# Two MLP units interleaved at the start of the up projection, transpositions by pairs of token tiles, activation sums on VectorE

## The reference, cut to what matters

```python
mod = silu(c) @ w_mod + b_mod                   # shift2, scale2, gate2 are columns of it
x1 = x + gate1 * rms_norm(mixed @ w_out, g_post_mix)
h  = rms_norm(x1, g_pre_mlp) * (1 + scale2) + shift2
u  = relu(h @ w_mlp_up)                         # 2048 x 8192
y  = (u * u) @ w_mlp_down                       # 8192 x 2048
out = x1 + gate2 * rms_norm(y, g_post_mlp)
```

## Time and profile before

| | us |
|---|---|
| median of 3 runs | 2401.2 |
| lowest, highest | 2395.54, 2403.61 |
| profiled execution, its own time | 2401.67 |
| its span, first to last instruction | 2399.9 |
| TensorE busy (matmuls) | 2303.2 (96%) |
| VectorE busy | 1453.2 (61%) |
| ScalarE busy | 901.2 (38%) |
| GpSimd busy | 597.2 (25%) |
| mean granted TensorE clock | 0.979 |

### The profile page before, as it was taken

The page is one execution under the profiler, slowest core; times in us unless marked ns, Lnnn a source line. Parts: engine busy times, 40 slices in busy tenths (PEclk is TensorE's granted clock), DMA queues, the critical chain, the costliest instruction groups (busy, mean ns, idle before and its releaser), DMA issues.

```text
span 2399.9 us, 33914 instructions
## 1 busy us (share of the span) xinstructions
PE 2303.2 (96%) x13028; PEld 1940.1 (81%) x13028; DVE 1453.2 (61%) x1820; ACT 901.2 (38%) x1167; POOL 597.2 (25%) x348
## 2 busy tenths in 40 slices
PE   6989999999988999779999999999999999999998
PEld 1558787887767788679999999999888888888886
DVE  6649883992349564777777777776544333333335
ACT  4334424222336422644444444444322223222222
POOL 6544453444347000100000000001999300000000
PEclk8999999999999999899999999999999999999999
DMA  8977664333232475223333333334766545444433
GB/s 311 359 272 256 235 247 98 89 96 97 79 102 84 141 294 206 88 106 132 132 131 131 132 131 131 132 134 149 263 222 217 168 139 194 143 136 140 144 118 140
DMA packets 129760, 391.21 MB, mean 163 GB/s; under 512 B 18320, under 2 KB 19984, under 8 KB 117520
## 3 DMA queue, kind: packets, MB, share of 16 engines
q1 hardware_dynamic: 115408, 347.65, 41.9%
q10 hardware_dynamic: 9664, 25.70, 2.7%
q0 software_dynamic: 4608, 16.78, 2.4%
HBM read 356.25 MB, written 33.57 MB: 162 GB/s over the span
## 4 chain that ended last, share of the span: by engine, by line
PE 92%; DVE 5%; ACT 1%; issue 1%; DMA 1%; POOL 0%; DVEq 0%; ACTq 0%; SPq 0%; PEldq 0%; POOLq 0%
PE psum L852 29%; PE psum L854 29%; PE psum L853 29%; PE psum L932 1%; PE psum L917 1%; DVE steps L1775 1%; PE psum L894 0%; DVE pt_lo L2067 0%; DVE probs L2054 0%; ACT h_raw L1579 0%; DVE q_lo L2014 0%; DVE T_lo L2196 0%; PE psum L940 0%; DMA bias_s<-bias_out 0%; DMA pos_qi<-in_pos_columns 0%
## 5 line engine op out<-in xcount | busy, mean ns | idle before, releaser
L2139 DVE TENSOR_TENSOR w_lo<-raw,w_hi 128x1024 fp32r<-128x1024 f32 x128 | 175.7, 1372 | 425.1 <-ACT w_hi L1541 425.1
L854 PE MATMUL psum<-w_hi,uin_lo 128*128 128x512 f32 x1024 | 406.9, 397 | 0.0
L852 PE MATMUL psum<-w_hi,uin_hi 128*128 128x512 f32 x1024 | 406.1, 397 | 0.0
L853 PE MATMUL psum<-w_lo,uin_hi 128*128 128x512 f32 x1024 | 403.4, 394 | 0.0
L758 POOL TENSOR_TENSOR w_lo<-raw,w_hi 128x1024 fp32r<-128x1024 f32 (+1 forms) x96 | 260.6, 2719 | 338.3 <-ACT w_hi L1275 338.3
L1541 ACT ACTIVATE w_hi<-raw 128x1024 fp32r<-128x1024 f32 x128 | 135.6, 1060 | 491.4 <-PE psum L854 475.9
L852 PE MATMUL psum<-T_hi,w_hi 128*128 128x256 f32 x1024 | 290.1, 283 | 20.3 <-DVE T_lo L2196 20.3
L853 PE MATMUL psum<-T_lo,w_hi 128*128 128x256 f32 x1024 | 289.4, 283 | 0.0
L854 PE MATMUL psum<-T_hi,w_lo 128*128 128x256 f32 x1024 | 289.3, 283 | 0.0
L1275 ACT ACTIVATE w_hi<-raw 128x1024 fp32r<-128x1024 f32 (+1 forms) x128 | 129.2, 1013 | 348.4 <-PE psum L854 319.7
L852 PE MATMUL psum<-h_hi,w_hi 128*128 128x512 f32 (+1 forms) x592 | 238.7, 403 | 6.7 <-issue 4.0
(11 more groups left out here) (307 smaller groups left out, 4318.7 us busy)
## 6 DMA issues: line engine op xcount, KB each, us to landing
raw<-in_w_mlp_down SPq DMA_DIRECT2D x128, 512.0 KB, 3.9
raw<-in_w_in SPq DMA_DIRECT2D x88, 512.0 KB, 3.7
mod_ring<-in_w_mod_first SPq DMA_DIRECT2D x32, 1024.0 KB, 8.8
mod_slab<-in_w_mod SPq DMA_DIRECT2D x32, 1024.0 KB, 5.3
raw<-in_w_up_units SPq DMA_DIRECT2D x64, 512.0 KB, 5.1
unit_odd<-in_w_up_units SPq DMA_DIRECT2D x64, 512.0 KB, 4.8
uin<-u_s SPq DMA_DIRECT2D x128, 256.0 KB, 4.2
raw<-in_w_out SPq DMA_DIRECT2D x32, 512.0 KB, 5.8
```

The source lines that it names most:

```text
L852: nc.tensor.matmul(o, a_hi, b_hi, start=first, stop=False)
L853: nc.tensor.matmul(o, a_hi, b_lo, start=False, stop=False)
L854: return nc.tensor.matmul(o, a_lo, b_hi, start=False, stop=last)
L2139: V.tensor_tensor(w_lo[:, slot, :, :], raw[:, slot, :, :], w_hi[:, slot, :, :].bitcast(F32), ALU.subtract).then_inc(down_lo, 1)
```

## The change

- The tables of products have another order: A11 with B11, A12 with B21, then S1 with T1, S4 with B22, S3 with T3, S2 with T2, A22 with T4. (n, m) below counts in it.
- At the start, units 0 and 1 are taken together in the order `START`, 14 products over banks given by hand (`START_BANK`); unit 2 waits for the combinations that free them (`COMB_AFTER_START`).
- Each x1 tile has its own root and diagonal: one `rsqrt` for tiles 0 and 1, one for 2, one for 3 (`x1_scales`). The transpositions go in four groups of 16: group 0 and 1 are tiles 0 and 1 with lower and upper feature tiles (B11, B21), group 2 and 3 tiles 2 and 3 (B12, B22). ScalarE reads quadrants, 256 wide, 32 reads in place of 16.
- All T sums are VectorE's. GpSimd has no work here.
- Weight sums are in place: S3 over A21, S2 over A11, S4 over A12, S1 in one of two buffers. P1 has two buffers; the combinations write straight into `u_st`; five of the seven come together after product 5 (the sixth).
- SyncE loads unit 1 once the output projection has ended, unit 2 after the low part of operand (0, 6).
- The start of the down projection asks for its banks in the order of the new products.

```diff
-OP_A = ("A11", "S1", "S2", "A12", "S3", "S4", "A22")
-OP_B = ("B11", "T1", "T2", "B21", "T3", "B22", "T4")
+OP_A = ("A11", "A12", "S1", "S4", "S3", "S2", "A22")
+OP_B = ("B11", "B21", "T1", "B22", "T3", "T2", "T4")
+SUMS = ("S1", "S3", "S2", "S4")
+T_SUMS = ("T1", "T3", "T2", "T4")
+TURNED = ("B11", "B21", "B12", "B22")
+START = ((0, 0), (0, 1), (1, 0), (1, 1), (0, 2), (1, 2), (0, 3), (1, 3), (0, 4), (0, 5), (0, 6), (1, 4), (1, 5), (1, 6))
+START_BANK = {(0, 0): 4, (0, 1): 5, (1, 0): 6, (1, 1): 7, (0, 2): 4, (1, 2): 5, (0, 3): 6, (1, 3): 7, (0, 4): 0, (0, 5): 1,
+              (0, 6): 2, (1, 4): 3, (1, 5): 0, (1, 6): 1}
+START_COMB = ((1, 3, 4, 5, 6, 7, 8), (2, 9, 10, 11, 12, 13, 14))
 N_SUMS = 4
 N_COMBS = 7
-COMB_OF = (0, 5, 1, 3, 4, 6, 7)
+COMB_OF = (0, 1, 5, 6, 3, 2, 7)
+COMB_AFTER_START = (9, 14, 8, 10, 6, 12, 7)
...
-        diag = at(32, "diag", [P, TT, P], F32)
+        diag = at(0, "diag", [P, TT, P], F32)
...
+        def place(n, m, i):
+            return START.index((n, m)) if at_start(i) and n < 2 else OPS * n + m
+        def operand(p, i):
+            return START[p] if at_start(i) and p < 2 * OPS else divmod(p, OPS)
+        def comb_no(n, k, i):
+            if at_start(i) and n < 2:
+                return START_COMB[n][k - 1]
+            return i * (BLOCK * N_COMBS) + (N_COMBS * n + k)
+        def op_bank(n, m, i):
+            b = START_BANK[n, m] if at_start(i) and n < 2 else m
+            return psum[:, 4 * (1 - TURN_HALF) + b if b < 4 else 4 * TURN_HALF + b - 4, 0:TOK]
+        def turn_bank(group, b):
+            return psum[:, 4 * (TURN_HALF if group == 1 else 1 - TURN_HALF) + b, :]
...
-            for t in range(TT):
+            def store_x1(t):
                 sp.wait_ge(x1_ready, t + 1)
                 sp.dma_start(x1_s[:, t, :], y1[:, t, :]).then_inc(x1_stored, 16)
-            load_quad(1, Q11)
-            load_quad(1, Q21)
-            sp.wait_ge(t_pool, 4)
-            load_quad(1, Q22)
-            load_quad(1, Q12)
-            for n in range(2, BLOCK):
-                load_unit(n, 0)
+            store_x1(0)
+            store_x1(1)
+            sp.wait_ge(slab_used, MLP0)
+            for qd in (Q11, Q12, Q21, Q22):
+                load_quad(1, qd)
+            store_x1(2)
+            store_x1(3)
+            sp.wait_ge(op_lo, START.index((0, OPS - 1)) + 1)
+            for qd in (Q21, Q22, Q11, Q12):
+                load_quad(2, qd)
+            load_unit(3, 0)
...
-            for hf in range(2):
-                k = slice(HALF // 2 * hf, HALF // 2 * hf + HALF // 2)
-                pool.wait_ge(h_full_ready, KD)
-                pool.wait_ge(t_ready, 2)
-                nc.gpsimd.tensor_tensor(h2_quad["T3"][:, k, :], h2_quad["B22"][:, k, :], h2_quad["B12"][:, k, :],
-                                        ALU.subtract).then_inc(t_pool, 1)
...
+            def turn(group):
+                first, kt0 = 2 * (group // 2), HALF * (group % 2)
+                if group == 0:
+                    pe.wait_ge(dve_freed, freed("D", STAGE["mod4"] + 1))
+                if group == 1:
+                    pe.wait_ge(act_freed, a0)
+                    pe.wait_ge(dve_freed, d0)
+                for t in range(first, first + 2):
+                    pe.wait_ge(diag_ready, t + 1)
+                    for kk in range(HALF):
+                        kt, b = kt0 + kk, kk // 2
+                        if group >= 2 and t == first and kk % 2 == 0:
+                            pe.wait_ge(h_full_ready, 2 * HALF * (group - 2) + 2 * b + 2)
+                        c = TOK * (kk % 2) + P * (t - first)
+                        last = nc.tensor.matmul(turn_bank(group, b)[:, c:c + P], y1[:, t, P * kt:P * kt + P], diag[:, t, :],
+                                                start=True, stop=True)
+                        if t > first and kk % 2:
+                            last.then_inc(turned, 1)
+            def product(n, m, i):
+                p = place(n, m, i)
+                pe.wait_ge(op_lo, i * (BLOCK * OPS) + p + 1)
+                if at_start(i) and n < 2:
+                    if (n, m) == (0, 0):
+                        pe.wait_ge(h_full_ready, 2 * HALF)
+                    elif START_BANK[n, m] < 4 and m < 5:
+                        pe.wait_ge(h_full_ready, 4 * HALF)
+                    elif (n, m) in ((0, 2), (0, 3)):
+                        pe.wait_ge(p1_ready, m - 1)
+                    elif (n, m) in ((1, 2), (1, 3)):
+                        pe.wait_ge(comb_ready, comb_no(m - 2, 1, 0))
+                    elif (n, m) == (1, 5):
+                        pe.wait_ge(comb_ready, comb_no(0, 3, 0))
+                    elif (n, m) == (1, 6):
+                        pe.wait_ge(comb_ready, comb_no(0, 2, 0))
+                elif at_start(i) and n == 2:
+                    pe.wait_ge(comb_ready, COMB_AFTER_START[m])
+                elif m == 0:
+                    pe.wait_ge(p1_ready, i * BLOCK + n)
+                else:
+                    pe.wait_ge(comb_ready, comb_no(n - 1, COMB_OF[m], i))
+                o = op_bank(n, m, i)
+                    if at_start(i) and n == 0 and k % (HALF // 2) == 0:
+                last.then_inc(op_used, 1)
...
-            pe.wait_ge(diag_ready, TT)
-            for kt in range(HALF + HALF // 2):
-                turn_x1(kt)
-            def turn_beside(k):
-                if k < HALF // 2:
-                    turn_x1(HALF + HALF // 2 + k)
-            product(0, 0, 0, after=turn_beside)
-            for m in range(1, OPS):
-                product(0, m, 0)
-            for n in range(1, BLOCK):
+                last.then_inc(op_used, 1)
+            turn(0)
+            turn(1)
+            turn(2)
+            product(0, 0, 0)
+            product(0, 1, 0)
+            turn(3)
+            for n, m in START[2:]:
+                product(n, m, 0)
+            for n in range(2, BLOCK):
...
-                for t in ((2, 3, 0, 1), (0, 1, 2, 3))[TURN_HALF]:
+                for nth, t in enumerate(((2, 0, 3, 1), (0, 2, 1, 3))[TURN_HALF]):
                     if j == 0:
-                        pe.wait_ge(comb_ready, N_COMBS * UNITS - {2 * TURN_HALF: 1, 2 * TURN_HALF + 1: 0}.get(t, 2))
+                        pe.wait_ge(comb_ready, N_COMBS * UNITS - (6, 4, 1, 0)[nth])
...
+            for kk in range(HALF // 2):
+                h_full_of(0, kk)
+            x1_squares(TT - 1)
+            for kk in range(HALF // 2, HALF):
+                h_full_of(0, kk)
+            b_high(0, 0)
+            b_high(0, 1)
+            for p in range(2):
+                op_high(*START[p], 0)
+            for kk in range(HALF):
+                h_full_of(1, kk)
+            b_high(1, 0)
+            b_high(1, 1)
+            for p in range(2, RING):
+                op_high(*START[p], 0)
+            for kk in range(HALF):
+                h_full_of(2, kk)
             for hf in range(2):
-                for k in range(HALF // 2 * hf, HALF // 2 * hf + HALF // 2):
-                    h_full_of(k)
-                b_high(0, hf)
-            for k in range(HALF, HALF + HALF // 2):
-                h_full_of(k)
-            for hf in range(2):
-                b_high(1, hf)
-            for k in range(HALF + HALF // 2, KD):
-                h_full_of(k)
-            after_product(0, 0, 0)
-            for m in range(2, OPS):
-                for hf in range(2):
-                    b_high(m, hf)
-                after_product(0, m - 1, 0)
-            after_product(0, OPS - 1, 0)
-            for n in range(1, BLOCK):
+                b_high(2, hf)
+            for p, (n, m) in enumerate(START):
+                after_product(n, m, 0)
+                if p == 2:
+                    for kk in range(HALF):
+                        h_full_of(3, kk)
+                if 2 <= p <= 5:
+                    for hf in range(2):
+                        b_high(p + 1, hf)
+                if p == START.index((1, 4)):
+                    finish_unit(0, 0)
...
-                    out, a, b, op = s_tmp[0][:], a21, a22, ALU.add
+                    if not at_start(i) or n >= 2:
+                        dve.wait_ge(op_lo, ops + OPS * n - 8)
+                    V.tensor_tensor(s1, a21, a22, ALU.add).then_inc(s_ready, 1)
                 elif k == 1:
-                    out, a, b, op = s_tmp[1][:], s_tmp[0][:], a11, ALU.subtract
+                    V.tensor_tensor(a21, a11, a21, ALU.subtract).then_inc(s_ready, 1)
                 elif k == 2:
-                    out, a, b, op = a21, a11, a21, ALU.subtract
+                    dve.wait_ge(op_lo, ops + place(n, 0, i) + 1)
+                    V.tensor_tensor(a11, s1, a11, ALU.subtract).then_inc(s_ready, 1)
                 else:
-                    dve.wait_ge(op_lo, ops + 2)
-                    out, a, b, op = s_tmp[0][:], a12, s_tmp[1][:], ALU.subtract
-                if k:
-                    dve.wait_ge(s_ready, at_)
-                V.tensor_tensor(out, a, b, op).then_inc(s_ready, 1)
```

(63 more changed lines are left out.)

261 lines of the change are left out of this document (102 added, 159 removed).

## The result

| | before | changed |
|---|---|---|
| median (lowest to highest) of 8 runs each, us | 2399.45 (2393.93 to 2406.62) | 2379.46 (2373.99 to 2389.08) |
| ratio, 95% interval | | 0.9924 (0.9904 to 0.9944) |
| profiled execution: own time, span | 2401.67, 2399.9 | 2383.34, 2381.5 |
| mean granted clock | 0.979 | 0.985 |

A second comparison, of 6 runs with 11 of the kernel before, gave 2381.28 against 2395.91, ratio 0.9937 (0.9919 to 0.9954): 14.6 us.

The account below looks back on a forecast made before the run. TensorE, busy 96%, bounds, with time to win in start-up holes behind other engines. The 21st product moves from 1088.4 to 1077.2, 11.2 us, taken as 10: 2401.2 becomes 2391.0 us, range 2385 to 2398.5.

Parts of the forecast that it names:

- ScalarE term: ScalarE's queue before product (0,0): 16.4 us from 977.4, reads 0.48 each; start at 993.9, 4.6 us before the old one.
- term of unit 2's weights: At unit 2's start: A11 lands at 1047.9, A12 at 1049.2; (2,0) starts at 1055.8 instead of 1053.0.
- subtraction of 1.3: On the whole start: the old queues laid out alike end 1.3 us too early, so 11.2 us gain became 10.
- The other price that the prediction gave: ScalarE's 256-wide reads under the Read-Write Bubble: if each cost its whole duration, the sum would be 3.1 us longer.
- All sums on VectorE: VectorE bounds from B22 on; moved T3 and T4 sums cost some 4.6 us; 14th product ends at 1053.1.
- But that alone gives little: Diagonals per tile: the 9.85 us hole shrinks to 1.1, with little gain alone because ScalarE becomes the first bound.
- rival 3: TensorE in the new start: half clock stays, 16 us slower, 2417.5; 4 in 100, shared with a loop acquiring waits.
- rival 4: At the start: more than laid out, the holes go and half clock with them, gain over 15 us; 5 in 100.
- signs of being wrong: Loop over 19.94 us a unit, first product after 996, VectorE instructions over 1.25 us, clock at 0.5 beyond 1045.

Follow-up runs that it names:

- B22 read earlier: Changed kernel with ScalarE reading B22's transpositions two weight operands earlier; stretch 96.43 us against 98.65.
- late loads: Kernel taking units 0 and 1 one after the other, with two of unit 1's weight quarters issued only after T4's sums; stretch 104.21 us against 97.80.
- three reorderings: Changed kernel with B22 read earlier, unit 1's last three weight sums before B22's low part, unit 2's quarters each behind its operand; stretch 91.77 us, ratio 0.9925 to before.
- units one after the other: Changed kernel with unit 0's seven products, then unit 1's, in place of interleaved; stretch 97.80 us against 98.65.
- one weight copy early: Kernel with three reorderings, one weight high part before the last tile's squares, unit 0's first weight sum after the first tile's addition; stretch 92.07 us against 91.77.

## Why the prediction was wrong

The time lies 11.5 us below the forecast of 2391.0. The sum was 4.3 too small: the ScalarE term, the term of unit 2's weights and the subtraction of 1.3 are the steps that failed, each about 1 us. The starting level was 1.75 too high. The remaining 5.7 (less 0.2 of rounding) are what this comparison's 20.0 holds beyond the stretch's 14.3. The second comparison has only 0.4 of it, so I take it for chance and no effect of the change. Without it 2379.5 would have been 2385.2, just inside the range.

*What bounds.* Right: the holes from (1, 3) on are released by VectorE, GpSimd is empty, the loop is unchanged (578.14 us from the 22nd product to the down projection in both profiled executions).

*The level.* The median of 3 runs that the forecast started from, 2401.2, was high: four groups of 8 to 11 runs of the same kernel gave 2394.4 to 2399.5. The forecast ratio was 2391.0 / 2401.2 = 0.9958; measured, 0.9924 and 0.9937.

*The sum.* Forecast 10, laid out 11.2, measured 14.3 on the stretch. These terms make 4.6 (0.2 comes off since the 22nd product of before starts at 1088.20, not 1088.4, and 0.1 by rounding). Times count from the projection's last matmul, 975.27 in the layout, 972.82 in the changed trace:

| step | laid out | measured | of it new |
|---|---|---|---|
| first product starts | 18.6 | 17.60 | 1.0 |
| (1, 3) starts | 48.8 | 47.07 | 0.7 |
| (0, 4), (0, 5), (0, 6) start | 57.0, 62.8, 66.4 | 55.09, 60.93, 64.49 | 0.2 |
| (2, 0) starts | 80.5 | 77.43 | 1.2 |
| 21 products done | 101.9 | 98.65 | 0.2 |
| subtracted as error of the layout | 1.3 | 0 | 1.3 |

- "ScalarE up to the first product": the term that was mis-sized is the new read, taken at 0.48 us, measured 0.45 (3.59 for eight). Sixteen lie ahead of the first product (0.5 of its 1.0; the chain also began 0.2 sooner, and squares with root took 2.2 twice, not 2.4), sixteen more ahead of B22's high part (0.5 of the next 0.7). The other price that the prediction gave, each read at its whole duration, is further off still: a read lasts 0.55 and the next starts 0.10 before its end. The Trainium skill (Advanced Engine Details and Errata, TRN2 Errata) has the memory latency exposed as a bubble between instructions; here no idle time shows between the reads, their records even overlap. (32 reads at 0.56 in place of 0.48 would have cost 2.6, not the 3.1 that the prediction has.) The same part took 1.8 us for the last 16 transpositions; they are recorded as 32 matmuls and last 3.49, from 997.71 to the start of (1, 0). That miss stayed hidden, since VectorE set the start of (1, 3).
- "All sums on VectorE": its durations held (2.35 for two, hole of 4.21 for 5 forecast). But "the price of moving the sums, some 4.6 us, lies on this path" was wrong as a price: left on GpSimd, they would have cost 1.15 more, not 4.6 less, by the longer instructions beside them. The 3.37 that I read in the earlier trace rows said so.
- "Unit 2's weights": SyncE's issue, 1.9 early like all before it, landed as laid out; VectorE's chain from A11's landing to (2, 0) took 6.8, not 7.9. In the second trace it took 7.5, with A12 landing 0.9 later in the stretch, and only 0.3 of this term's 1.2 is left: the landing of the weights sets it.
- "The old queues laid out in the same way end 1.3 us too early, so I take 10": an error of the old layout doesn't carry over to a new order whose waits are others. This is the largest single miss.

*"But that alone gives little"*, of the diagonals, is the step whose reason failed although its number came near. The first product came 5.7 us earlier than before, and 8.3 earlier than in the new order with the old wait. I counted the hole and not what stands behind it: transpositions at half clock and a bank to be filled. With the 6.4 of unit 1's weights it comes to the size of the change, 7.9 + 6.4 = 14.3; that the two meet it so closely is partly luck, since the smaller prices (1.15, and the net of the rest) cancel.

*Rivals.* None came true. The half clock of rival 3 fell and rose as the rows above show (0.50 from 1020, 1.00 from 1034); rival 4, over 15, is where the first comparison stands and the second doesn't. The range failed from below: its lower end took a spread from three runs. On the scale of the layout the first product came at 992.9 (994 told) and the 21st ended at 1073.9 (1077 to 1079 told); none of the signs of being wrong appeared.

## What to carry to other kernels

Price each part by putting its old form back alone into the new kernel: here two parts, the diagonals and the early loads, carried nearly everything, and interleaving nothing that shows. A removed wait is worth the start-up behind it too (clock, first bank), not only the hole. One semaphore for several transfers makes the first operand wait for the last of them; and where VectorE hands a sum to ScalarE and gets it back, an instruction that needs neither belongs in between.

## What I had not expected

The units' loop has two paces at the same granted clock, whatever the kernel. From the 22nd product to the down projection it took 578.14 us in ten of the fourteen traces and 571.65 in the other four (B22 read earlier, late loads, three reorderings, and the second trace of the changed kernel). Here is 1150 to 1600 in the kernel with the units one after the other, then in the second trace of the changed one (columns of the earlier trace rows):

```profile
1150.00:1600.00 450.00, 450.00 (x3795) 450.00 (x3794) 350.32 (x409) 218.14 (x227) 0.00 (x0) 1.00 0.35 130
```
```profile
1150.00:1600.00 450.00, 450.00 (x3837) 450.00 (x3836) 353.85 (x410) 219.71 (x229) 0.00 (x0) 1.00 0.35 132
```

3837 matmuls against 3795, 1.1% more, both at 1.00. The down projection likewise took 722.2 or 723.8, and the output projection's last matmul started anywhere from 967.81 to 977.72 (the last from the kernel with one weight copy early; 975.41 is the latest of the twelve traces whose TensorE program and weight copies ahead of it are the same). Together these make up most of the spread between executions of one kernel, 9 to 15 us in most groups of runs, and they are why a difference of 7 us has to be read in the stretch where it arises. The quicker pace shortens the stretch by some 0.3 us, an estimate from products at 2.82 in place of 2.85. Both paces occur on both chips that the record names for the runs. What sets the pace stays open.
